# Second layer's modulation computed in the first layer's expert opening, with the weights as stationary operand

## The reference

```python
for l in range(DEPTH):                                   # DEPTH = 2
    m_lat = (jax.nn.silu(c) @ ada_w[l] + ada_b[l])       # ada_w[l] is 1024 x 6144
    m_ctx = jax.nn.silu(c_ctx) @ ada_w[l] + ada_b[l]
    u_lat, u_ctx = modulate(x, sh1, sc1), modulate(xc, ch1, cs1)
    ...                                                  # token mixers, w_out, layer norm
    x = layer_norm(ALPHA * x + g2 * peer_ffn(modulate(x, sh2, sc2), P))
```

## Time and profile before

| | us |
|---|---|
| three runs, median (lowest to highest) | 6590.27 (6570.46 to 6602.92) |
| the profiled execution | 6602.0 |
| its span, first to last instruction | 6599.9 |
| TensorE matmul busy | 5369.8 (81%) |
| VectorE busy | 3593.7 (54%) |
| GpSimd busy | 1892.8 (29%) |
| ScalarE busy | 1470.7 (22%) |
| mean granted TensorE clock | 0.855 of full speed |

### The profile page before, as it was taken

The page is one execution under the profiler, slowest core; times in us unless marked ns, Lnnn a source line. Parts: engine busy times, 40 slices in busy tenths (PEclk is TensorE's granted clock), DMA queues, the critical chain, the costliest instruction groups (busy, mean ns, idle before and its releaser), DMA issues.

```text
span 6599.9 us, 64371 instructions
## 1 busy us (share of the span) xinstructions
PE 5369.8 (81%) x22991; PEld 3630.2 (55%) x22991; DVE 3593.7 (54%) x7828; ACT 1470.7 (22%) x3637; POOL 1892.8 (29%) x2020
## 2 busy tenths in 40 slices
PE   8899877968553499999998889987796643999997
PEld 3699444737452355555554369954474533566664
DVE  1554172726653497776665255415363753676655
ACT  1100032212354311111111110003221264111111
POOL 0000000000479755445552000000000199334542
PEclk9899978688765599999999889998767855999998
DMA  6000101004235599999996500010001345999996
GB/s 210 17 1 1 35 4 32 1 32 150 93 122 212 211 400 400 388 384 382 388 389 254 165 17 1 1 35 7 29 1 64 115 150 195 393 407 407 408 403 274
DMA packets 292958, 1184.06 MB, mean 179 GB/s; under 512 B 24736, under 2 KB 106912, under 8 KB 207392
## 3 DMA queue, kind: packets, MB, share of 16 engines
q0 software_dynamic: 92160, 671.13, 25.6%
q1 hardware_dynamic: 194864, 455.59, 19.4%
q10 hardware_dynamic: 5616, 53.23, 1.9%
HBM read 1130.57 MB, written 49.28 MB: 179 GB/s over the span
## 4 chain that ended last, share of the span: by engine, by line
PE 63%; DVE 15%; DMA 8%; ACT 8%; issue 5%; POOL 1%; ACTq 0%; DVEq 0%; SPq 0%; POOLq 0%
PE psum L495 62%; DMA arena<-in_ut 6%; DVE arena L1337 3%; ACT y_features L1047 3%; ACT arena L971 2%; DMA arena<-gate_blocks 2%; ACT y_features L1049 1%; DVE arena L1656 1%; DVE arena L1731 1%; DVE arena L1346 1%; DVE arena L1340 1%; DVE arena L1476 1%; DVE u_features L1343 1%; DVE x_tokens L1337 1%; DVE arena L1474 1%
## 5 line engine op out<-in xcount | busy, mean ns | idle before, releaser
L495 PE MATMUL psum<-arena 128*128 128x64 f32 (+6 forms) x8416 | 1550.2, 360 | 46.9 <-DVE arena L1656 23.8
L495 PE MATMUL psum<-u_features,weight_ring 128*128 128x256 f32 (+2 forms) x4672 | 1337.7, 444 | 20.7 <-DVE u_features L1343 11.6
L495 PEld LDWEIGHTS psum<-arena 128*128 128x128 f32 (+2 forms) x8416 | 1082.6, 212 | 397.6 <-issue 277.2
L495 PEld LDWEIGHTS psum<-u_features,weight_ring 128*128 128x128 f32 x4672 | 911.7, 197 | 442.7 <-issue 222.5
L1300 POOL TENSOR_SCALAR y_features<-consts 128x128 f32<-128x128 f32 x640 | 660.4, 1041 | 304.3 <-ACT consts L1037 231.7
L495 PE MATMUL psum<-y_features 128*128 128x128 f32 x1280 | 315.9, 425 | 510.3 <-issue 322.0
L971 ACT ACTIVATE arena<-psum 128x512 f32<-128x512 f32 (+5 forms) x404 | 251.8, 623 | 1801.6 <-PE psum L495 1576.9
L1315 POOL TENSOR_TENSOR arena<-consts 128x1 f32<-128x1 f32 x640 | 296.5, 463 | 1213.7 <-DVE y_features L1560 1059.8
L495 PE MATMUL psum<-u_features,arena 128*128 128x384 f32 (+1 forms) x2048 | 584.9, 440 | 46.2 <-DMA arena<-in_ut 43.0
L495 PE MATMUL psum<-weight_ring,consts 128*128 128x512 f32 x1280 | 575.0, 596 | 13.0 <-DVE consts L1547 13.0
L495 PEld LDWEIGHTS psum<-y_features 128*128 128x128 f32 x1280 | 273.9, 316 | 551.3 <-issue 340.2
(11 more groups left out here) (200 smaller groups left out, 5543.1 us busy)
## 6 DMA issues: line engine op xcount, KB each, us to landing
weight_ring<-in_ws SPq DMA_DIRECT2D x250, 512.0 KB, 3.6
weight_ring<-in_ut SPq DMA_DIRECT2D x128, 512.0 KB
weight_ring<-in_uv SPq DMA_DIRECT2D x128, 512.0 KB
arena<-in_ut SPq DMA_DIRECT2D x128, 512.0 KB
arena<-in_uv SPq DMA_DIRECT2D x128, 512.0 KB
gate_blocks<-arena ACTq DMA_DIRECT2D x20, 2048.0 KB
arena<-gate_blocks SPq DMA_DIRECT2D x32, 768.0 KB
arena<-gate_blocks SPq DMA_DIRECT2D x32, 512.0 KB
```

What stands on the lines that cost most here:

```text
L495: return pe.matmul(o, w, x, start=first, stop=last, skip_group_check=True)
```

## The change

The modulation of both layers is computed the other way round. A piece of `ada_w` now holds the 1024 input rows of 128 outputs (`feature_pieces`), its eight 128 x 128 blocks are the stationary side, and the two conditioning columns are the moving side, two wide. The result is in column form at once: no rows, no `MR`, no turning. The first layer's 48 pieces stay at the start of the kernel. The second layer's 48 pieces are taken in the first layer's opening: they are due from 114.0 to 142.2 in the sorted list, behind the second pair's pieces and ahead of `exp` of tile 1 and of `turn`. They go to PSUM bank 7, and ScalarE copies them to the new buffer `MCN` at the place of the last of them in its list. The second layer then takes `MC` from `MCN`.

```diff
-PIECES = [ADA + RW + AQK + AV + HF + HT + WO + WQ * len(q) for q in QUERIED]
+PIECES = [(2 * ADA if l == 0 else 0) + RW + AQK + AV + HF + HT + WO + WQ * len(QUERIED[l]) for l in range(DEPTH)]
...
+        MCN = sb("next_mod_cols", 96)
...
-        MR = [take(512)[0:2, :] for _ in range(2)]
...
+            for n in range(ADA if l == 0 else 0):
+                events.append((114.0 + 0.6 * n, "ada", n, 0))
...
+            def ada_piece(b, n):
+
+                w = piece_ready()
+                for k in range(KB):
+                    ins = mm(bank(b, 2 * n, 2 * n + 2), w[:, k * P:(k + 1) * P], CC[:, 2 * k:2 * k + 2], k == 0, k == KB - 1)
+                piece_done(ins)
...
                 if l == 0:
                     pe.wait_ge(*at("cond silu"))
+                    for n in range(ADA):
+                        ada_piece(6, n)
+                    marks[("ada cols", 0)] = ("piece_used", piece[0])
                 else:
                     pe.wait_ge(*at("final", l - 1, NT - 1))
-                for c in range(ADA // 4 + 1):
-                    if c < ADA // 4:
-
-                        if c >= 2:
-                            pe.wait_ge(*at("ada rows kept", l, c - 2))
-                        for n in range(4):
-                            w = piece_ready()
-                            for j in range(2):
-                                k = 2 * n + j
-                                ins = mm(bank(5 + 2 * (c % 2))[0:2, :], CC[:, 2 * k:2 * k + 2], w[:, j * 512:(j + 1) * 512],
-                                         k == 0, k == KB - 1)
-                            piece_done(ins, "ada rows", l, c)
-                    if c:
-
-                        pe.wait_ge(*at("ada rows kept", l, c - 1))
-                        for j in range(4):
-                            n = 4 * (c - 1) + j
-                            ins = mm(bank(6, 2 * n, 2 * n + 2), MR[(c - 1) % 2][:, j * P:(j + 1) * P], ident[0:2, 0:2])
-                        done(ins, "ada turned", l, c - 1)
...
+                    if kind == "ada":
+                        ada_piece(7, n)
+                        marks[("ada cols", 1)] = ("piece_used", piece[0])
...
-                for c in range(ADA // 4):
-                    act.wait_ge(*at("ada rows", l, c))
-                    if c >= 2:
-                        act.wait_ge(*at("ada turned", l, c - 2))
-                    copy(MR[c % 2], bank(5 + 2 * (c % 2))[0:2, :], "ada rows kept", l, c)
-
...
+                    if kind == "ada" and n == ADA - 1:
+                        act.wait_ge(*at("ada cols", 1))
+                        copy(MCN[:], bank(7, 0, 96), "next ada cols")
...
-                dve.wait_ge(*at("ada turned", l, ADA // 4 - 1))
-                tt(MC[:].rearrange("p (n s) -> p n s", s=2), bank(6, 0, 96).rearrange("p (n s) -> p n s", s=2),
+                dve.wait_ge(*(at("next ada cols") if l else at("ada cols", 0)))
+                tt(MC[:].rearrange("p (n s) -> p n s", s=2), (MCN[:] if l else bank(6, 0, 96)).rearrange("p (n s) -> p n s", s=2),
                    spread(COL[:, C_ADAB:C_ADAB + ADA], 2), ALU.add)
...
-        pieces += [token_pieces(g["ada_w"][l][:, c:c + 512]) for c in range(0, 6 * D, 512)]
+        pieces += [feature_pieces(g["ada_w"][0])] if l == 0 else []
...
-                   *[feature_pieces(g["peer_wq"][l]) for _ in QUERIED[l]]]
+                   feature_pieces(g["peer_wq"][l]), feature_pieces(g["peer_wq"][l]),
+                   *([feature_pieces(g["ada_w"][1]), feature_pieces(g["peer_wq"][0])] if l == 0 else [])]
```

More of the change, by code:

```diff
@@ L59 @@
 PARTS = 2 * HALF + 2
-ARENA = 24472
+ARENA = 24376
 ADA, RW, AQK, AV, HF, HT, WO, WQ = 48, 7, 8, 4, 6, 4, 8, 16
-PIECES = [ADA + RW + AQK + AV + HF + HT + WO + WQ * len(q) for q in QUERIED]
+PIECES = [(2 * ADA if l == 0 else 0) + RW + AQK + AV + HF + HT + WO + WQ * len(QUERIED[l]) for l in range(DEPTH)]
 C_CONV, C_A0, C_W0, C_KK, C_KA, C_RK, C_ADAB = 0, 18, 20, 24, 26, 28, 30
```

## The result

Four executions of the changed kernel have a median of 6680.31 us (6662.54 to 6702.37), four of the kernel before run beside them on the same chip 6580.36 (6567.97 to 6602.92). The ratio is 1.0156 [1.0124, 1.0189]: slower by some 100 us. The predicted 6702 was 22 us too high, inside its range (6668 to 6740) and on the right side.

The account below looks back on a forecast made before the run. The prediction read TensorE as carrying 63% of the chain and VectorE 15%. Its terms, 63.5 + 124.2 - 76.2 = +111.5 us on a median of 6590.3, gave 6702 us, range 6668 to 6740.

Parts of the forecast that it names:

- Price of a record: Each of a layer's 768 modulation records, with two moving columns, costs 0.2133 us at a granted clock of 0.50.
- Rival 4: A modulation record costs up to 0.256 us, 33 us more for each layer: 6768; chance 0.04.
- Which clock: Both new modulation streams are granted 0.50, except the first 3.0 us of the opening's stream at full rate.
- Rivals 1 and 2: Full clock granted to both new streams (6547, chance 0.05), or kept in the opening only (6625, chance 0.03).
- Layer one's start: Layer one's first projection starts at 194.9 in place of 131.44: +63.5 us.
- The opening: Layer two's modulation, moved into layer one's opening, ends at 1811.4 and makes the turn late by +124.2 us.
- Rival 3: The turn's delay is taken up behind it, 1689 to 1895 us: 6578 if all, 6640 if half; chance 0.04.
- Layer two's start: Without modulation products there, layer two's first projection starts at 3688.6 in place of 3764.75: -76.2 us.
- The rest: The 24 copies to `MR` on ScalarE go; they ran beside the products, and no term was added for them.

Follow-up runs that it names:

- e3: Changed kernel with layer one's modulation wide as before and layer two's 48 pieces one behind each gate group from dense tile 2 on; 6521.86 us, ratio to before 0.9901.
- e4: Changed kernel with 64 moving columns in place of two in the first layer's modulation; 6679.15 us, ratio to before 1.0152.
- e5: Changed kernel with two dummy products 512 columns wide added to each piece of the first layer's modulation; 6829.64 us, one execution.
- e9: Changed kernel with 128 moving columns in place of two in both layers' modulation; 6521.28 us, ratio to before 0.9901.
- e10: Changed kernel with 64 moving columns in the opening's stream only, two in the first layer's; 6631.88 us, one execution.
- e1: Changed kernel with the first layer's modulation back in its old wide form, the second's as changed; 6613.4 us, ratio to before 1.0043.
- e8: Changed kernel, layer one wide as before; layer two's pieces 11 ahead of the turn, 37 behind groups from dense tile 2's 21st on; 6494.62 us, ratio to before 0.9859.
- e6: Kernel before with an unused 96-column buffer ahead of the arena and the arena 96 columns shorter; 6573.52 us, ratio to before 0.9969.
- e11: Kernel before with an unused 96-column buffer behind the arena and the arena 96 columns shorter; 6566.06 us, one execution.
- e7: Kernel before, unchanged, profiled once more; 6591.14 us, one execution.
- e2: Changed kernel with both layers' modulation in the old wide form, the second's still moved into the opening; 6555.86 us, ratio to before 0.9952.

## Why the prediction was right, point by point

*Price of a record.* 0.2133 was forecast, 0.2135 and 0.2130 (156.70 / 736) measured. The row it came from, `rwkv bonus` with two moving columns, is the same instruction form, and so its price held to the third digit over a stream 30 times as long. Rival 4, up to 0.256 by the gate products, fell, and it rested on a misread row: the 2.05 us of a group run from the start of its first record to the end of its last. Among others the same records cost no more than narrow ones: in e3 8 of 128 columns and 16 of two take 1927.63 - 1922.51 = 5.12 us, 0.2133 each.

*Which clock.* Right for the changed kernel: half in both streams, the full clock for 3.2 us at the start of the opening's stream where I gave it 3.0. Rivals 1 and 2 fell. The reason I gave, that being busy doesn't win the full clock for light products, holds by e4 and e5 beyond what I had rows for. But I would not have forecast the rest by it: the streams with 64 columns (e4) and with half of their time in 512 wide products (e5) stayed at half, the one with 128 columns rose (e9), and by e10 the product alone doesn't give the answer. The Trainium skill's advice to keep TensorE continuously busy, "TensorE: Matmul & The Clock Gate", section "Why this matters for your kernels", agrees with e9 and disagrees with the changed kernel and e4, where 164 us without a gap stayed at the half clock's pace (0.2135 and 0.2136 us a record), and with the opening's stream, granted 0.50 for 156.7 us; the measurement decides.

*Layer one's start.* First projection forecast at 194.9, seen at 195.15. e1 put the whole term on the first layer's form.

*The opening.* Products to 1811.4 and turn +124.2 forecast; +123.8 seen, and e1, with nothing late ahead of it, had them end at 1811.57 and turn at 1813.20. The chain ran as written: last record, copy, `exp` behind it in ScalarE's list, turn. Nothing of it was given back: turn to blocks took 574.7 us for 575.9. Rival 3 fell. Its argument for, GpSimd idle between turn and 1895, was idle time that waits for the turn, and e3 shows how tight the groups are: 48 pieces of 3.41 us between them cost 19.7 us in all. e8 shows the cover that was really there: 38.6 us ahead of the turn and the stretch in which GpSimd is full, 3 to 6 us for the whole modulation.

*Layer two's start.* -76.2 forecast and -76.2 seen.

*The rest.* Here the prediction was wrong by 23 us in the sum of 111.5 (88.6 by the spans): I set everything behind layer two's projection at nothing, and the second layer's blocks took 20.9 us less. The diff showed the step: a buffer of 384 bytes goes in ahead of the arena, and I costed it only for what is written to it. By e6 and e11 its place alone makes the difference. The -5.1 us of the first layer's blocks belong to the one profiled execution of before and not to the change. In e7, the same kernel, the first block product and the first product of layer two's modulation are
```profile
2262.56 7.92 PE L495 MATMUL psum<-u_features,weight_ring 128*128 128x384 f32 x18 [0.94 <-ACT arena L971]
...
3645.66 6.83 PE L495 MATMUL psum<-weight_ring,cond_cols 128*2 128x512 f32 x12 [44.76 <-DVE x_tokens L1337]
```
which is 1383.1 us where before has 3652.68 - 2265.01 = 1387.7 and the changed kernel 1382.6. The +2.1 and +2.3 us in the mixers are less than these vary among the fourteen traces: 1389 to 1404 us in layer one, where e2 and e3, both 1404, stand apart from the rest (up to 1394) for a reason that wasn't followed, and 1814 (e11) to 1849 us (e6) in layer two.

*The level of the runs.* Of the 22 us by which 6702 was too high, 10 are the median of before, which was 6590.27 when I predicted and 6580.36 in the comparison. The profiled execution of before is at the top of its runs (6602.0), that of after 10 us above its median. By spans the change costs 88.6 us, by medians 100; I can't say which of the two is nearer, since the interval reaches from 82 to 124 us.

## What to carry to other kernels

A weights-stationary product with few moving columns cost its weight load here, and that at the clock that the stream got (0.213 us a record at 1.2 GHz, 0.11 at 2.4 GHz): look for a row of the same form and take its level from there, not from how busy the engine will be. Moved work is hidden only as far as idle time of its engine reaches at the new place; spread it over the stretches where another engine is full, and look which instruction in the queue stands behind each new wait. Where a stage is bound by DMA, a new small buffer ahead of the large ones isn't neutral: set its place against a kernel that only has the buffer.

## What the runs showed of the hardware

- *The granted clock has a memory.* It goes by the level before as well as by the product. 64 columns begun from the half clock: 0.2136 us a record for all 768 (e4). Begun from the full clock: 0.111 for 416 records, up to a gap of 1.74 us, and 0.214 for all 352 behind it (e10, one trace). The stream with two columns was down to 0.50 after 3.2 us (changed kernel); the one with 128 columns began at the half clock's pace and doubled it after some 6 us (e9). An estimate from e10: what a single late piece can cost is 352 x 0.103 = 36 us.
- *A wide record pays the level of its stream.* 512 columns take 0.85 us among narrow ones (e5), 0.44 among their like (7.03 / 16).
- *The mixers carry most of the difference between e11 and before.* From layer two's projection to its blocks the fourteen traces take 1814 to 1849 us, though no variant changes an instruction of the mixers, and 17 executions of before alone range over 35 us (6571.04 to 6605.65). Window of e11 and of before over them, 1300 us (columns as above): the same work is granted 0.87 once and 0.84 the other time, and 81 more records fit in.
```profile
3900.00:5200.00 1300.00, 1097.50 (x6429) 857.41 (x6428) 627.31 (x1652) 220.69 (x404) 34.77 (x41) 0.87 0.10 32
```
```profile
3900.00:5200.00 1300.00, 1103.89 (x6348) 862.52 (x6348) 601.22 (x1526) 215.48 (x385) 34.83 (x41) 0.84 0.09 29
```
- *Placement moves a DMA-bound stage by 2%.* With 384 bytes ahead of the arena 415 to 419 GB/s and 969 to 974 us in nine traces (977 and 978 in two more, e2 at 411 GB/s), without them 407 to 409 GB/s and 991 to 993 us; the same bytes behind it: nothing (990.7).
